# Attention rounds in slots of at most 512 keys for two heads at once

## What is computed

```python
q, k, v, gate = split(rmsnorm(h) @ w_in)        # for A and for B
# A: softmax over the keys of three dilated windows
s = (q @ k.T) * hd ** -0.5;  p = exp(s - max(s));  o_A = (p @ v) / sum(p)
# B: for the keys s < t
z = (q @ k.T) * hd ** -0.5
between = reversed_cumsum(log_sigmoid(-z)) - log_sigmoid(-z)
o_B = exp(log_sigmoid(z) + between) @ v
h = h + (sigmoid(gate_a) * (o_A @ w_up_a) + sigmoid(gate_b) * (o_B @ w_up_b)) @ w_out
h = h + memory_attention(h);  h = h + swiglu(h);  out = rmsnorm(h)
```

## Time and profile before

| | us |
|---|---|
| median of 3 runs | 1957.56 (1952.74 to 1957.62) |
| the profiled execution | 1952.04 |
| its span, first to last instruction | 1949.9 |
| PE busy | 1835.7 (94%) |
| DVE busy | 1121.2 (58%) |
| ACT busy | 601.7 (31%) |
| POOL busy | 537.6 (28%) |
| the four rounds | 111.0 to 864.5 |

### The profile page before, as it was taken

The page is one execution under the profiler, slowest core; times in us unless marked ns, Lnnn a source line. Parts: engine busy times, 40 slices in busy tenths (PEclk is TensorE's granted clock), DMA queues, the critical chain, the costliest instruction groups (busy, mean ns, idle before and its releaser), DMA issues.

```text
span 1949.9 us, 24701 instructions
## 1 busy us (share of the span) xinstructions
PE 1835.7 (94%) x8578; PEld 1475.8 (76%) x8578; DVE 1121.2 (58%) x1684; ACT 601.7 (31%) x1024; POOL 537.6 (28%) x296
## 2 busy tenths in 40 slices
PE   5699999999999999969999889999999999999995
PEld 5577777777777777757887767888888888888884
DVE  8547894788478957986544565333333433343336
ACT  3324852485247525763212333000000000000003
POOL 5321112111211220213332112333333333333335
PEclk9899999999999999979999989999999999999998
DMA  5311111111111110145312001111111111111112
GB/s 218 101 36 39 38 45 61 40 38 44 61 40 38 44 60 29 49 168 197 119 52 89 22 18 48 43 45 53 43 54 43 54 43 53 43 43 54 43 43 86
DMA packets 43238, 118.71 MB, mean 61 GB/s; under 512 B 6160, under 2 KB 14608, under 8 KB 43024
## 3 DMA queue, kind: packets, MB, share of 16 engines
q1 hardware_dynamic: 21312, 75.66, 11.6%
q10 hardware_dynamic: 21840, 41.96, 6.4%
HBM read 97.67 MB, written 18.87 MB: 60 GB/s over the span
## 4 chain that ended last, share of the span: by engine, by line
PE 73%; DVE 16%; issue 5%; ACT 4%; ACTq 1%; DMA 1%; DVEq 0%; POOL 0%; SPq 0%; POOLq 0%
PE ps L358 63%; PE ps L472 4%; DVE e_row L1260 4%; DVE e_row L1259 2%; PE ps L503 2%; PE ps L488 2%; DVE pt L1244 1%; DVE rms L1125 1%; ACT pt L843 1%; DVE raw L1158 1%; ACTq L801 1%; DVE h L1469 1%; DVE raw L1174 1%; ACT n_hi L969 0%; DVE h L1329 0%
## 5 line engine op out<-in xcount | busy, mean ns | idle before, releaser
L324 POOL TENSOR_SCALAR w_hi<-w_stage 128x1024 fp32r<-128x1024 f32 x138 | 149.9, 1086 | 1380.2 <-issue 686.2
L358 PE MATMUL ps<-n_hi,w_hi 128*128 128x512 f32 x1536 | 396.2, 398 | 27.2 <-DVE raw L1158 16.2
L358 PE MATMUL ps<-n_lo,w_hi 128*128 128x512 f32 x1536 | 389.9, 395 | 0.0
L358 PE MATMUL ps<-n_hi,w_lo 128*128 128x512 f32 x1536 | 387.9, 393 | 0.0
L326 POOL TENSOR_TENSOR w_lo<-w_stage,w_hi 128x1024 fp32r<-128x1024 f32 x138 | 366.4, 2655 | 11.5
L358 PEld LDWEIGHTS ps<-n_hi,w_hi 128*128 128x128 f32 x1536 | 285.8, 190 | 94.5 <-DVE raw L1158 22.6
L358 PEld LDWEIGHTS ps<-n_lo,w_hi 128*128 128x128 f32 x1536 | 287.9, 190 | 60.0
L358 PEld LDWEIGHTS ps<-n_hi,w_lo 128*128 128x128 f32 x1536 | 285.3, 188 | 58.1
L1329 DVE TENSOR_TENSOR h<-ps,h 128x512 f32<-128x512 f32 (+1 forms) x192 | 132.0, 690 | 156.9 <-PE ps L358 156.5
L1024 ACT ACTIVATE a_hi<-u_f 128x1024 fp32r<-128x1024 f32 x22 | 23.4, 1062 | 475.4 <-DVE u_f L1435 475.4
L1427 DVE TENSOR_TENSOR u_f<-ps,rms 128x512 f32<-128x512 f32 x44 | 30.4, 691 | 205.3 <-PE ps L358 205.3
(11 more groups left out here) (168 smaller groups left out, 2221.4 us busy)
## 6 DMA issues: line engine op xcount, KB each, us to landing
w_stage<-weights_in SPq DMA_DIRECT2D x138, 512.0 KB, 3.3
gates_scratch<-raw ACTq DMA_DIRECT2D x16, 512.0 KB, 2.8
o_scratch<-o_sum ACTq DMA_DIRECT2D x128, 32.0 KB, 1.8
n_lo<-o_scratch ACTq DMA_DIRECT2D x8, 512.0 KB, 5.0
g_a<-gates_scratch ACTq DMA_DIRECT2D x8, 512.0 KB, 3.7
g_b<-gates_scratch ACTq DMA_DIRECT2D x8, 512.0 KB, 4.5
h<-x_t_in ACTq DMA_DIRECT2D x8, 512.0 KB, 9.0
out_t<-h ACTq DMA_DIRECT2D x16, 256.0 KB, 2.1
```

The source lines that it names most:

```text
L324: pool.tensor_scalar(w_hi[:, b, :], stage[:, b, :], 1.0, 1.0, ALU.mult, ALU.mult).then_inc(w_rounded, 1)
L358: ins = pe.matmul(bank, w[:, b, c:c + P], mv(k), start=(first and n == 0), stop=(last and n == total - 1))
```

## The change

A slot now holds a chunk: a block of queries, both heads, and at most four blocks of keys (512). Blocks 0 to 3 have one chunk, blocks 4 to 7 two (the one with the diagonal first), so A and B have 12 each and a round 24 chunks in 28 slots (36 slots before). `opens(s)` is a query block's first chunk, `closes(s)` its last. Elementwise work takes both heads in one instruction of up to 1024 columns, apart from the maximum, the exponential of A with its sum, and B's running sum, which stay one for each head (a second chunk starts from the first one's carry). A's scaling by the inverse goes from DVE to ACT (`normalise`). POOL's two instructions for a weight tile become two and four.

```diff
--- before.py
+++ after.py
@@ -50,11 +50,42 @@
-UNITS = 32
-ORDER = ([(h, b) for b in range(NB) for h in range(2)]
-         + [(h, b) for b in reversed(range(NB)) for h in range(2)])
+def chunks_of(mixer, blocks):
+    return [(mixer, b, c, min(4, b + 1 - c)) for b in blocks for c in reversed(range(0, b + 1, 4))]
+CHUNKS = chunks_of("A", range(NB)) + chunks_of("B", reversed(range(NB)))
+N_CHUNKS = len(CHUNKS)
+N_A = N_CHUNKS // 2
 LAG = 3
-SLOTS = UNITS + 4
+SLOTS = N_CHUNKS + LAG + 1
+QUERIES = 2 * NB
+def width(s):
+    return CHUNKS[s][3] * P
+def opens(s):
+    _, b, c, n = CHUNKS[s]
+    return c + n == b + 1
+def closes(s):
+    return 0 <= s < N_CHUNKS and CHUNKS[s][2] == 0
+def query(s):
+    return sum(closes(r) for r in range(s))
+def siblings(s):
+    return [s] if opens(s) else [s - 1, s]
...
+                if s in at:
+                    self.fill[s].insert(1, (n, at.index(s), None))
+                    self.turned[s] = (n, at.index(s))
...
-                then("dve", s + 3, "rope", n, 0, 1)
-                then("dve", s + 4, "rope", n, 2)
-                then("act", s + 5, "hi", n)
-                then("dve", s + 6, "lo", n)
+                then("dve", s + 3, "rope", n, 0, 1, 2)
+                then("act", s + 4, "hi", n)
+                then("dve", s + 5, "lo", n)
...
-ROUND = Plan(("VB", "KB", "QB", "G0", "G1", "QA", "KA", "VA", "G2", "G3"),
-             [2] * 9 + [1] * 9 + [2] * 4 + [1] + [2] * 10 + [1, 1, 2], {"TB": 4, "TA": 30})
+ROUND = Plan(("VB", "KB", "QB", "QA", "KA", "VA", "G0", "G1", "G2", "G3"),
+             [2] * 12 + [3] * 8 + [2] * 4 + [1] * 4, {"TB": (4, 5), "TA": (17, 19)})
 LAST = Plan(("VB", "KB", "QB", "G0", "G1", "G2", "G3"),
-            [2] * 6 + [1] * 12 + [2] * 7 + [1] * 4 + [0] * 7, {"TB": 4})
+            [2] * 21 + [0] * 7, {"TB": (4, 5)})
...
+        ps_t = ps[:, 4:6, :].rearrange("p h (n q) -> p h n q", q=P)
+        ps_v = ps[:, 6:8, 2 * P:4 * P].rearrange("p b (n q) -> p b n q", q=P)
...
-                pool.tensor_scalar(w_hi[:, b, :], stage[:, b, :], 1.0, 1.0, ALU.mult, ALU.mult).then_inc(w_rounded, 1)
+                for part in range(2):
+                    at = blk(part, HALF)
+                    ins = pool.tensor_scalar(w_hi[:, b, at], stage[:, b, at], 1.0, 1.0, ALU.mult, ALU.mult)
+                ins.then_inc(w_rounded, 1)
                 pool.wait_ge(w_rounded, number)
-                pool.tensor_tensor(w_lo[:, b, :], stage[:, b, :], w_hi[:, b, :].bitcast(F32),
-                                   ALU.subtract).then_inc(w_split, 1)
+                for part in range(4):
+                    at = blk(part, 2 * P)
+                    ins = pool.tensor_tensor(w_lo[:, b, at], stage[:, b, at], w_hi[:, b, at].bitcast(F32), ALU.subtract)
+                ins.then_inc(w_split, 1)
```

More of the change, by code:

```diff
@@ L809, in v_hi @@
                 act.wait_ge(vt_full, number)
[L810 to L812 removed]
+                for b in range(2):
+                    ins = act.activation(v_of[m][:, blk(2 * half + b, 2), :, 0, :],
+                                         ps_v[:, b, :, :].rearrange("p n (h d) -> p n h d", h=2), ACT.Copy)
+                ins.then_inc(vt_hi_s, 1)
             for n, name in enumerate(("QA", "KA")):
@@ new lines, in round_ @@
+                    u = s - LAG - 1
+                    if closes(u):
+                        act.wait_ge(av_full, i * QUERIES + (query(u) + 1))
+                        act.activation(o_low[:, query(u) % 2, :, :], ps[HD:P, 6:8, 0:P], ACT.Copy).then_inc(o_low_s, 1)
+                    if N_A <= s - 2 < N_CHUNKS:
+                        weights_of(s - 2)
+                    if closes(s - 1) and s - 1 < N_A:
+                        normalise(s - 1)
+                    if s in plan.turned:
+                        name, half = plan.turned[s]
+                        v_hi(name[1], half, i * 4 + (SPLIT_NUMBER[name] + half))
@@ L867, in round_ @@
+                    if closes(s) and s < N_A:
+                        exponentials(s)
+                    if N_A <= s < N_CHUNKS:
+                        softplus_rest(s)
                     for what, name, *rest in plan.after["act"][s]:
                         unit = plan.units.get(name)
-                        if what == "v_hi":
-                            v_hi(name[1], rest[0], i * 4 + (SPLIT_NUMBER[name] + rest[0]))
-                        elif what == "swap":
+                        if what == "swap":
@@ L1146, in _ @@
             step(dve.memset(swap[:], 0.0))
-            for b in range(4):
-                dve.memset(o_of(b), 0.0).then_inc(o_out[b], 16)
+            for b in range(2):
+                dve.memset(o_sum[:, b, :, :], 0.0).then_inc(o_out[b], 16)
             for b in range(2):
@@ L1262, in round_ @@
+                    if s in plan.turned:
+                        name, half = plan.turned[s]
+                        v_lo(name[1], half, i * 4 + (SPLIT_NUMBER[name] + half))
                     for what, name, *rest in plan.after["dve"][s]:
                         unit = plan.units.get(name)
-                        if what == "v_lo":
-                            v_lo(name[1], rest[0], i * 4 + (SPLIT_NUMBER[name] + rest[0]))
-                        elif what == "rope":
+                        if what == "rope":
```

271 lines of the change are left out of this document (92 added, 179 removed).

## The result

The changed kernel takes 1942.34 us (median of 7 runs, 1938.62 to 1944.29) against 1954.71 (7 runs, 1948.10 to 1957.62): ratio 0.994, 95% interval 0.9923 to 0.9957, 0.6% faster. Forecast was 1922. The profiled execution is 1942.34 us long, its span 1940.5.

A forecast was written before the change was run, and what follows sets the result against it. PE, busy 94% of the span, was taken to bound the kernel. From 1952.0 us profiled, -29 (three full rounds, -10 each) and -4 (last round) gave 1919, named 1922 for the median; forecast band 1910 to 1930, range 1897 to 1945.

The forecast's parts named there:

- At once: Logits products of the two heads, on different 64-row halves of PE, run concurrently: 10 us saved a full round.
- 3 us of switching: Groups of 64-row products on PE fall from 32 to 24 a round, at 0.40 us each: 3.2 us less.
- Rival (a): Logits products of the two heads do not run at once, only switching is saved: 1938 us; 1930 to 1948, chance 0.26.
- The slot-17 wait: PE stalls 5.5 us before V's transposes in slot 17, waiting for o_sum, with about 1.5 us of half clock behind.
- Slots 0 to 11 of the last round 69 us: Length of the last round's first twelve slots, part of its 162 us against 165.8 before.
- Slots 12 to 19 58: These last-round slots take 58 us, each o_sum standing 1.2 us in attend's way every second slot.
- From slot 20 to the last attend 35: End of the last round, walked along DVE with the rounding of o between: 35 us.
- Stalls: about 14 us against 11: PE's stalls in a full round, after the change against before: +3.5 us in the round's sum.
- rival (b): Attend and V's transposes behind o_sum, slots 13 to 19, cost more than PE saves: slower, above 1963 us, chance 0.11.
- The sign that I had named for this: The forecast is wrong if PE idles in slots 12 to 19 by more than 15 us.
- Zero in the sum: POOL's extra instructions in FFN and projections, perhaps 0.3 us a tile, hidden under 11 us of matmuls: zero counted.
- At the head 1 us: At the kernel's head, where the first w_lo is on the chain, POOL's pieces cost 1 us.

The follow-up runs named there:

- e5: Changed kernel with PE waiting for head 0's last logits product before head 1's first, three products per head in sequence: 2003.20 us, ratio 1.0252 to the kernel before.
- e6: Changed kernel with ACT's o_low ahead of the rounding and DVE's two o_sum additions ahead of the lo part and difference: 1913.28 us, ratio 0.9789 to before.
- e1: Changed kernel with POOL's two whole instructions for a weight tile instead of pieces: 1962.86 us, ratio 1.0047 to the kernel before.
- e4: Changed kernel with A's transposes of V in slots 24 and 25 instead of 17 and 19: 1930.92 us, ratio 0.9891 to the kernel before.
- e7: Changed kernel with POOL's whole instructions for the first ten weight tiles and pieces from then on: 1930.94 us, ratio 0.9884 to the kernel before.
- e3: Changed kernel with head 0's three logits products issued before head 1's three, without a wait between: 1942.29 us, ratio 0.9943 to the kernel before.

## Why the prediction was off, step by step

The direction held, and 1942 lies at the upper end of the range of 1897 to 1945. The size did not: the sum said -33 us on the profiled execution, and it moved -10. Of the 23 us between, 8.5 are the head, 9 the three full rounds and 6 the last one.

- **"At once", 10 us a round, and 3 us of switching: right together.** 0.89 us for six products, issue 187 to 172; the traces don't part the pairs from the switching. e5 shows that what PE loses reaches the end. Rival (a), no pairs at once, would have given 1938 and lies nearer to the measured time than the forecast does, and it is false: a total alone would have confirmed the wrong mechanism.
- **The slot-17 wait, 5.5 + 1.5 us: right.** 6.0 us, and half clock behind it.
- **Slots 0 to 11 of the last round 69 us: right** (68.3). **Slots 12 to 19 58: 57.8, by luck.** Seven of them take 6.1 to 6.6 us, with no wait for `o_sum` where I had put 1.2 in every second one. Slot 14 takes 12.6: PE stands there for 4.22 us behind `o_sum` (774.11), with half clock behind it. DVE itself had stood 5.17 us for ACT just before, which made A's last normalising and B's first softplus terms in turn. e6 has slot 14 at 11.4 us, so the order of `o_sum` is the smaller part of it.
- **"From slot 20 to the last attend 35": 42.** I walked these slots by DVE's and ACT's own durations, and did not chain each narrow attend to `o_sum` behind ACT's rounding, lo part and difference. The timeline has that wait before five of the last six attends (4.69 to 1.87 us), and PE runs at half clock between them: eight attend matmuls take 2.05 us, in slot 21 1.17. With `o_sum` first these slots take 34.5 us (e6).
- **"Stalls: about 14 us against 11": 18.7 against 8.5.** What I left out are attends of slots 14, 16, 22 and 25 behind `o_sum` (0.55 to 1.29 us each), and more half clock, behind slot 17 and the loop's turn. This and the last slots are one step, and it is the one that failed: the prediction noted `o_sum` "last in a longer slot" under rival (b) and priced little but V's transposes behind it. e6 measures the order, 29 us. Rival (b) was thus right in mechanism, and stayed below the point from which it decides. The sign that I had named for this, over 15 us of PE idle in slots 12 to 19, did not show it: 8.8 us stand there in the second round, and the rest in places that I did not watch.
- **"Zero in the sum" for POOL: wrong twice.** "At the head 1 us", itself left out of the sum, was 8.5: a tile in pieces takes 8.1 us against a busy DVE, where the whole one took 4.7, and PE waits for it there ([3.21], [1.59]). And the relief of DVE, which I mentioned for single instructions, was given no term: it is 24 us over the four rounds (e1). The two errors have opposite signs; without the pieces my sum would have been off by 40 us (the profiled execution of e1, 1959.15, against 1919), not by 23.

So the gain went to a new wait (29 us) and to the head (8 to 11), and was partly paid back by POOL's pieces. Not settled: why e4, e6 and e7 add up so fully, how much of the rounds' loss is half clock that the waits bring with them, and whether e5's 61 us holds more than the serial products and the wait.

## What to carry to other kernels

On an engine that runs in order, the instruction that frees a PSUM bank for TensorE belongs first in its slot, and it is priced by all the work ahead of it, not by its own length: two DVE instructions of 0.41 us, moved with ACT's of 0.38 ahead of 2.4 us of DVE's work and 1.0 of ACT's, gave 29 us here, and put last in the slot such instructions cost 157 in the kernel before. When a change joins or lengthens the work of a slot, ask for every wait of the bounding engine what now stands ahead of its releaser, in the narrow slots too. GpSimd's instructions have a price on VectorE that depends on their length; cut them where VectorE is tight and leave them whole where GpSimd is the chain.

## What the runs showed of the hardware

- Products of the two 64-row halves run at once even when three of one half are issued before three of the other: 0.89 us for six in turns, 0.90 for three and three, against 1.59 on one half alone. The Trainium skill has such matmuls starting about 4 ns apart ("TensorE: Matmul & The Clock Gate", Part 3). The traces agree for products in turns (3 or 4 ns in most pairs); with three and three the pairs start 10 or 11 ns apart in most (e3).
- GpSimd's short pieces: four of 256 columns take 2.80 us undisturbed, where one of 1024 takes 2.4, and 4.95 against a busy VectorE, where it takes 3.2. In the second round VectorE is held by 0.54 us at most, instead of 2.0 and more.
- Behind an idle of 6.0 us TensorE ran its next eight matmuls at 1.2 GHz (3.76 us instead of 2.0). The length of the idle does not tell it alone: in the kernel before eight matmuls behind 1.50 us ran at 1.2 GHz too (3.44 us), and eight behind 2.17 us did not (2.11).
